# A decoder trunk on one core: experts sorted by load, the four smallest in half-width unsplit products

## What is computed

```python
D_FF = 3584; N_EXPERTS = 8; TOP_K = 2
def swiglu(h, wg, wu, wd):
    return (jax.nn.silu(h @ wg) * (h @ wu)) @ wd
def moe_swiglu(h, router, wg, wu, wd):
    logits = (xt @ router).astype(jnp.float32)          # 256 tokens x 8 experts
    topv, topi = lax.top_k(logits, TOP_K)
    gates = jax.nn.softmax(topv, axis=-1)
    ...
    xb = xpad[row_tok].reshape(n_blocks, MOE_BLOCK, d)  # tokens grouped by expert
    yb = lax.map(expert_block, (xb, block_expert))      # swiglu with that expert's weights
    y = (yb.reshape(n_rows, d) * row_gate[:, None]).astype(h.dtype)
    out = jnp.zeros((t + 1, d), h.dtype).at[row_tok].add(y)[:t]
```

## Time and profile before

| | us |
|---|---|
| three runs | 1573.34, 1575.76, 1575.86 |
| median | 1575.76 |
| profiled execution | 1574.27 |
| its span, first to last instruction | 1572.4 |
| busy: PE, VectorE, ScalarE, GpSimd | 1555.0, 1264.7, 1073.2, 81.7 |
| expert stage, first to last product | 613.84 to 1564.65 |

### The profile page before, as it was taken

The page is one execution under the profiler, slowest core; times in us unless marked ns, Lnnn a source line. Parts: engine busy times, 40 slices in busy tenths (PEclk is TensorE's granted clock), DMA queues, the critical chain, the costliest instruction groups (busy, mean ns, idle before and its releaser), DMA issues.

```text
span 1572.4 us, 28661 instructions
## 1 busy us (share of the span) xinstructions
PE 1555.0 (99%) x10958; PEld 1360.2 (87%) x10958; DVE 1264.7 (80%) x1448; ACT 1073.2 (68%) x1323; POOL 81.7 (5%) x82
## 2 busy tenths in 40 slices
PE   8999999999999999999999999999999999999997
PEld 8989999999998898888888888888888888888886
DVE  5686754444558867999999999999999999999996
ACT  5545544444446455888888888888888888888885
POOL 0022000000000400000000000000000000000000
PEclk9999999999999999999999999999999999999999
DMA  8700555555344017999999999999999999999994
GB/s 314 235 2 3 229 198 177 178 184 188 123 182 134 3 38 301 394 372 358 400 381 353 416 381 351 401 381 347 419 382 348 402 382 358 399 385 360 397 379 153
DMA packets 66808, 447.76 MB, mean 285 GB/s; under 512 B 8208, under 2 KB 10784, under 8 KB 14112
## 3 DMA queue, kind: packets, MB, share of 16 engines
q1 hardware_dynamic: 63344, 434.46, 71.7%
q0 software_dynamic: 2688, 9.44, 2.8%
q10 hardware_dynamic: 688, 2.62, 0.5%
HBM read 438.63 MB, written 6.29 MB: 283 GB/s over the span
## 4 chain that ended last, share of the span: by engine, by line
PE 96%; DVE 2%; ACT 1%; issue 1%; DMA 0%; POOL 0%; SPq 0%; DVEq 0%; ACTq 0%; POOLq 0%
PE bank L790 28%; PE bank L792 27%; PE bank L791 27%; PE bank L771 9%; PE bank L1465 2%; ACT w_hi L1544 0%; DMA ring<-in_w_in 0%; PE bank L961 0%; PE bank L811 0%; PE bank L1428 0%; PE bank L1214 0%; DVE w_lo L1986 0%; PE bank L1106 0%; POOL out L741 0%; ACT arena L1544 0%
## 5 line engine op out<-in xcount | busy, mean ns | idle before, releaser
L1544 ACT ACTIVATE w_hi<-ring 128x1024 fp32r<-128x1024 f32 x812 | 858.1, 1061 | 328.4 <-PE bank L792 320.3
L2247 DVE TENSOR_TENSOR w_lo<-ring,w_hi 128x1024 fp32r<-128x1024 f32 x672 | 813.5, 1224 | 60.5 <-ACT w_hi L1544 11.3
L790 PE MATMUL bank<-w_hi,acts_hi 128*128 128x512 f32 (+1 forms) x1376 | 538.9, 392 | 0.2 <-DVE w_lo L2247 0.2
L792 PE MATMUL bank<-w_hi,acts_lo 128*128 128x512 f32 (+1 forms) x1376 | 533.1, 387 | 0.0
L791 PE MATMUL bank<-w_lo,acts_hi 128*128 128x512 f32 (+1 forms) x1376 | 532.3, 387 | 0.0
L792 PEld LDWEIGHTS bank<-w_hi,acts_lo 128*128 128x128 f32 x1376 | 258.4, 188 | 53.6
L790 PEld LDWEIGHTS bank<-w_hi,acts_hi 128*128 128x128 f32 x1376 | 258.6, 188 | 51.6 <-DVE w_lo L2247 0.9
L791 PEld LDWEIGHTS bank<-w_lo,acts_hi 128*128 128x128 f32 x1376 | 258.7, 188 | 50.7
L790 PE MATMUL bank<-acts_hi,w_hi 128*128 128x256 f32 x884 | 252.5, 286 | 1.8 <-DVE acts_lo L2176 0.8
L791 PE MATMUL bank<-acts_lo,w_hi 128*128 128x256 f32 x884 | 250.1, 283 | 0.0
L792 PE MATMUL bank<-acts_hi,w_lo 128*128 128x256 f32 x884 | 250.0, 283 | 0.0
(11 more groups left out here) (247 smaller groups left out, 1113.2 us busy)
## 6 DMA issues: line engine op xcount, KB each, us to landing
ring<-in_moe_wg SPq DMA_DIRECT2D x112, 1024.0 KB, 6.5
ring<-in_moe_wu SPq DMA_DIRECT2D x112, 1024.0 KB, 6.4
ring<-in_moe_wd SPq DMA_DIRECT2D x112, 1024.0 KB, 6.8
ring<-in_w_in SPq DMA_DIRECT2D x24, 1024.0 KB, 7.1
ring<-in_dense_wg SPq DMA_DIRECT2D x14, 1024.0 KB, 4.7
ring<-in_dense_wu SPq DMA_DIRECT2D x14, 1024.0 KB, 4.8
ring<-in_dense_wd SPq DMA_DIRECT2D x14, 1024.0 KB, 4.8
ring<-in_w_o SPq DMA_DIRECT2D x8, 1024.0 KB, 6.3
```

The lines of the kernel that those rows point to most:

```text
L790: pe.matmul(out_, a_hi, b_hi, start=first, stop=False, **kw)
L792: return pe.matmul(out_, a_lo, b_hi, start=False, stop=final, **kw)
L1544: return act.activation(o, i, ACT.Copy, **kw)
L2247: TT(w_lo[:, q, :], raw, w_hi[:, q, :].bitcast(F32), ALU.subtract).then_inc(lo_ready, 1)
```

## The change

The experts are ordered on chip by their load: expert 0 first, whatever its load (its weights are already being loaded when the order is known), then by falling load. They are taken in four pairs. The first of a pair (expert 0 and the three fullest) is computed as before, with 128 seats. The second (the four emptiest) gets 64 seats, and its products take the float32 weights as they are in the ring and unsplit activations. The stationary operand has 64 columns then, and two products stand side by side in the array: g in columns 0 to 63 and u in 64 to 127, each into its half of the partitions of one bank; and for the down products the two halves of the output columns. SyncE loads g and u of such an expert alternately, half by half, since PE uses them together, and a slot is free when PE has read it (`raw_read`). Which expert's weights are loaded is read by SyncE from `order_id` in SBUF. An expert that doesn't fit into its seats sets `flag`, and `over_pass` takes all eight again. The four pairs are a loop of three passes and a last pair.

```diff
+        EXPERT_B = []
+        for _j in range(NJ):
+            EXPERT_B += [(kind, _j, hf) for hf in range(2) for kind in "gu"]
+            EXPERT_B += [("d", _j - 1, hf) for hf in range(2) if _j]
+        EXPERT_B += [("d", NJ - 1, hf) for hf in range(2)]
...
+            def pair_pass():
+                for r in range(PAIRS):
+                    e = sp.value_load(order_id[0:1, 2 * r:2 * r + 1], min_val=0, max_val=NE - 1) if r else 0
+                    for i in range(PER_E):
+                        if i >= SLOTS:
+                            sp.wait_ge(lo_ready, MOE0 + r * PIECES_E + 2 * (i - SLOTS + 1))
+                        elif r:
+                            sp.wait_ge(raw_read, r * PER_E + i - SLOTS + 1)
...
+                        load_expert(e, i)
+                    if r == 0:
+                        sp.wait_ge(flag_ready, 1)
+                    e = sp.value_load(order_id[0:1, 2 * r + 1:2 * r + 2], min_val=0, max_val=NE - 1)
+                    for i in range(PER_E):
+                        if i >= SLOTS:
+                            sp.wait_ge(raw_read, r * PER_E + i - SLOTS + 1)
...
+                        load_expert(e, i, EXPERT_B)
...
+            def half_columns(j, hf, seen):
+
+                slots = []
+                for kind in "gu":
+                    i = place_b[(kind, j, hf)]
+                    pe.wait_ge(ring_in[e_slot[i]], seen.fills + e_count[i])
+                    slots.append(half_cols(e_slot[i]))
+                for k in range(4 * hf, 4 * hf + 4):
+                    for g, w in enumerate(slots):
+                        last_ = pe.matmul(bank[j % 2][g * C:(g + 1) * C, :], xb[:, k, :], w[:, k % 4, :],
+                                          start=k == 0, stop=k == KT - 1, skip_group_check=True)
+                last_.then_inc(raw_read, 2)
...
+            def down_rows(j, hf, seen):
+
+                i = place_b[("d", j, hf)]
+                pe.wait_ge(ring_in[e_slot[i]], seen.fills + e_count[i])
+                for q in (2 * hf, 2 * hf + 1):
+                    w = half_rows(e_slot[i])[:, q % 2, :]
+                    for g in range(2):
+                        last_ = pe.matmul(bank[4][g * C:(g + 1) * C, :], act_t[j % 2][:, q, :],
+                                          w[:, g * CW:(g + 1) * CW], start=j == q == 0, stop=j == NJ - 1 and q == 3,
+                                          skip_group_check=True)
+                last_.then_inc(raw_read, 1)
+
+            def half_chunks(seen):
+
+                for j in range(1, NJ):
+                    half_columns(j, 0, seen)
+                    turn_half(j - 1, seen)
+                    half_columns(j, 1, seen)
+                    pe.wait_ge(ac_ready, seen.acts + j)
+                    down_rows(j - 1, 0, seen)
+                    if j == NJ - 1:
+                        turn_half(j, seen)
+                    down_rows(j - 1, 1, seen)
+
+            def pair(r, last_one):
+
+                full, half_ = full_seen(r), half_seen(r)
+                full_chunks(full)
+                turn_half_slots(r * 32 + 16)
+                down(NJ - 1, full)
+                pe.wait_ge(ga_kept, half_.turned_x + 1)
+                for hf in range(2):
+                    half_columns(0, hf, half_)
+                pe.wait_ge(yg_kept, full.outs + 2)
+                half_chunks(half_)
+                if not last_one:
+                    turn_slots(full_seen(r + 1), r * 32 + 32)
+                pe.wait_ge(ac_ready, half_.acts + NJ)
+                for hf in range(2):
+                    down_rows(NJ - 1, hf, half_)
+                if not last_one:
+                    column_chunk("g", 0, full_seen(r + 1))
+                    column_chunk("u", 0, full_seen(r + 1))
+                    pe.wait_ge(yg_kept, half_.outs + 1)
```

More of the change, by code:

```diff
@@ L1 @@
+from collections import namedtuple
 from contextlib import ExitStack
@@ L66 @@
 N_PARAM = _at
+PAIRS = NE // 2
+Seen = namedtuple("Seen", "pieces fills turned_x low_x acts turned turned_kept silus outs experts halves raws")
 def constant_tables():
@@ L1775, in dense_split, with split @@
                         hi_ready, 1)
-            def split(kind, j, at1, pieces=range(4)):
+            def split(kind, j, seen, pieces=range(4)):
                 for q in pieces:
@@ new lines, in keep_out @@
+            def keep_out(seen, halved=False):
+                if not halved:
+                    act.wait_ge(pc_free, seen.pieces + (MOE0 + PIECES_E + PIECES))
+                act.wait_ge(gate_ready, seen.experts + 1)
+                act.wait_ge(to_set, seen.experts + 1)
+                for hf in range(2):
+                    if halved and hf == 0:
+                        act.wait_ge(half_done, 1)
+                    if halved and hf:
+                        act.wait_ge(pc_free, seen.pieces + (MOE0 + PIECES_E + PIECES))
+                    act.activation(yg[:, hf * 512:(hf + 1) * 512], bank[4 + hf][:, :], ACT.Identity,
+                                   scale=gate_e).then_inc(yg_kept, 1)
@@ new lines, in keep_half_out, with pair @@
+            def keep_half_out(seen):
+                act.wait_ge(raw_read, seen.halves + PER_E)
+                act.wait_ge(gate_ready, seen.experts + 1)
+                act.wait_ge(to_set, seen.experts + 1)
+                act.activation(yb, bank[4][:, :], ACT.Identity, scale=gate_e).then_inc(yg_kept, 1)
+            def pair(r, last_one):
+                full, half_ = full_seen(r), half_seen(r)
+                full_chunks(full)
+                half_x(half_)
+                keep_out(full)
+                keep_raw(0, half_)
+                for j in range(1, NJ):
+                    half_silu(j - 1, half_)
+                    keep_raw(j, half_)
+                half_silu(NJ - 1, half_)
+                if not last_one:
+                    gathered(full_seen(r + 1))
+                    split("g", 0, full_seen(r + 1))
+                keep_half_out(half_)
+                if not last_one:
+                    split("u", 0, full_seen(r + 1))
+                    silu(0, full_seen(r + 1))
```

685 lines of the change are left out of this document (402 added, 283 removed).

## The result

The changed kernel takes **1548.3 us** (median of four runs, 1547.4 to 1549.4) against 1575.3 us: a ratio of 0.983, interval 0.981 to 0.985. It is faster by 27 us where 67 were forecast. The sign was right, and so was what bounds a half expert; two fifths of the size came.

A forecast was written before the change was run, and what follows sets the result against it. PE bounds the kernel and loads follow it. Four pairs of about 219.5 us (878), plus 4.7 at the start and 1.7 at the end, make 885 for a 950.8 us stage: 66 off 1574.27 gives 1508 us, range 1485 to 1535 (0.63).

The forecast's parts named there:

- what bounds a half expert: In each 64-seat expert, loads set the pace: 105 us of loads against 79 us of PE work.
- forecast 420: Load rate taken for the 64-seat experts: 420 GB/s, read where loads caught up in the old trace.
- restart (3.2): After a 64-seat expert the ring is empty, so PE stands about 3.2 us before the next 128-seat expert.
- Rival (a): In 64-seat experts the two column groups don't overlap: 1716 us, slower; chance 0.09 together with all of Rival (b).
- Rival (b): PE's clock falls in 64-seat experts: 1530 to 1550 us if mixed; all of it, with Rival (a), 0.09.
- Rival (d): An expert with 64 seats has more tokens, so a second pass over eight runs: 948 us more; chance 0.01.
- rival (c): Loads hardly faster than before: 1538 us at 400 GB/s, 1572 at 381 (no change, 0.03), 1594 at 372 (worst, 0.03).
- the full part: The 128-seat expert of a pair, at PE's pace: 118.5 us, 121.7 with PE's standstill at its start.
- the scatters: Writing rows out at expert boundaries slows the loads: 1.4 us for each scatter, two in a pair.
- the queue is idle for 3: In the 128-seat expert's 121.7 us the ring lets some 46 loads through, 118.7 us, leaving the queue idle for 3.
- The sum: Time of a pair in terms of loads: 216.3 us with scatters, plus idle queue, about 219.5; bounds 216 and 227.
- the start: In the first expert PE waits once for VectorE's added ordering and gate steps: 4.7 us, bounds 0 and 6.

The follow-up runs named there:

- run 5: Changed kernel with both products of each pair in the 64-seat experts on the same 64 columns instead of side by side: 1727.2 us, 1.097.
- run 4: Changed kernel with every second gate, up and down product of the 64-seat experts left out, loads and waits kept: 1532.5 us, 0.973.
- Run 6: Changed kernel with the 64-seat expert's row transposes and first 16 products moved ahead of the preceding expert's last down products on TensorE: 1539.2 us, 0.977.
- run 1: Changed kernel with the loop over pairs written out on TensorE, ScalarE and VectorE: 1534.0 us, 0.974.
- run 2: Changed kernel with the loop over pairs written out on TensorE alone: 1534.9 us, 0.976.
- Run 3: Kernel before the change, with TensorE's loop over single experts made to hold two per turn: 1585.4 us, 1.007.
- run 8: Kernel of run 1 with the work that orders the experts removed, so they run as 0 to 7: 1529.6 us, 0.973.
- run 7: Changed kernel with the edits of run 1 and Run 6 together: 1532.2 us, 0.975.
- Run 12: Changed kernel with run 1's and Run 6's edits, order steps behind every second split, later TensorE waits and slot products, two more throwaway products: 1520.6 us, 0.966.

## Why the prediction was right and wrong

**Right: what bounded the kernel, and what would bound a half expert.** Loads at 412 to 421 GB/s in half experts (forecast 420), PE busy 80% there (75 to 85), records 0.22 us apart in a shared group, g and u side by side (run 5), 2.3 to 3.1 us of idle PE at the restart (3.2), half the splits. Rival (a) was priced at 1716 and measured at 1727. Rival (b) was rightly small: the clock did fall in some groups, to 0.91 to 0.96 over a half expert, and in run 4, with half of the products, 0.77 cost no load time. Such a group, behind a wait for its load, took 5.35 us for 3.65:

```profile
771.29 5.35 PE L1593 MATMUL bank<-ring,arena 128*64 128x512 f32 x16 [2.53 <-DMA ring<-in_moe_wu]
```

The Trainium skill warns of a low clock in groups of products that are shorter than the wait for their load ("TensorE: Matmul & The Clock Gate", HAM oscillation — how this bites in real kernels). Here the group is longer than its wait, 3.65 against 2.53 us, and yet some groups ran slow; it cost no load time. Rival (d) didn't happen, and rival (c) not as it was put: the half expert's slots were enough for 421 GB/s. The Trainium skill's 358 GB/s for one core ("DMA: Bandwidth & Descriptors", Specifications), by which the time would have been 1632 by the prediction's estimate, is not what this core drew. The 425 that the same page of the Trainium skill has for a core alone (Bandwidth) is near the 421 of the trace.

As a mean over a whole pair, though, the loads ran at 89.7 MB in 232.3 us, or 386 GB/s. So the time fell among 1535 to 1570, which had a chance of 0.18, for loads at 390 to 402 or a falling clock; what was lost was lost in the full part and at the hand-over, which no rival named. Rival (c)'s times are also added up unevenly: 1538 at 400 GB/s has the scatters in it, 1572 at 381 has not, and would be 1583 with them.

**Wrong: "the queue is idle for 3".** This is the term that was mis-sized most: with the scatters 5.8 us of load time were to be lost in a pair, and 18.9 were, of which some 5 go with the jump, told below. A full part was to let 46 loads through. But when PE restarts at 851.39, two of them have landed already, or just then. ScalarE's first two splits of g come from one load and the next two from another:

```profile
848.95 2.00 ACT L1695 ACTIVATE w_hi<-ring 128x1024 fp32r<-128x1024 f32 x2 [3.55 <-DMA ring<-in_moe_wg]
851.42 2.01 ACT L1695 ACTIVATE w_hi<-ring 128x1024 fp32r<-128x1024 f32 x2 [0.47 <-DMA ring<-in_moe_wg]
```

And 120 us at 383 GB/s are 46.0 MB, fewer than 44 loads. That this is why the full part lost so much was argued, and no run tested it. The other place was tested. Behind VectorE's last split of the full expert (739.9) no slot comes back until PE's first raw read of the next (748.6):

```profile
737.51 2.36 DVE L2445 TENSOR_TENSOR w_lo<-ring,w_hi 128x1024 fp32r<-128x1024 f32 x2 [0.24 <-ACT w_hi L1695]
746.47 0.15 DVE L2775 COPY arena<-arena 128x1 f32 x1 [6.59 <-ACT arena L2089]
```

Two loads are queued for 8.7 us, and the queue runs dry. The sum counted slots and forgot when each is given back. By the stretches 8.3 us of load time go in that place in the second pair. Run 6 filled most of the gap and got 2.3 and 3.9 us in the second and third pair for it, so not all of the lost load time was lost time: the full part is still at PE's pace.

**Missing: the jump.** No step of the sum looked at the length of TensorE's loop body, which the change made a third longer (637 to 864 instructions). It costs a stall of 3.6 to 4 us at two boundaries and a low clock behind it (0.79 over the 8 us from 866 and from 1098, where run 1 has 1.00): 14.2 us by the median of run 1, 13.4 by run 2's. The periods name 5.4 and 4.9 of it; 2.8 more in run 1's trace are the gather at the start, which varies between traces of the same code there. Run 3 lost 10 us by two such jumps. So some 10 of the 40.2 us missing in the stage are the jump's, the largest single piece that a run recovered.

**Too small, by the traces: the start.** 4.7 us forecast, of which 4.2 for what run 8 leaves out; 7.4 by its trace, but 4.4 by the medians and 1.7 by the ratios. The waits were about right, the clock that falls behind a wait wasn't counted. The stage also begins 1.15 us later (614.99 for 613.84).

With the jump and the gap gone a pair takes 223 to 225 us, 3.5 to 5.4 over the forecast. In run 7 the loads keep 393 GB/s for 120 us and 350 for the next 16, so 10.4 us of load time are still lost there where the sum had 5.8; no run took that apart. Run 12, with all edits, has a stage of 898.3 us (610.55 to 1508.81): of the 40.2 us missing 26.3 are won back, by runs that each had a cause in view, and 13.9 stay open.

## What to carry to other kernels

When a kernel hands over from one consumer of a ring to another, write down when each slot is given back, not how many there are: a pause in the giving back shows up in the load rate one queue length later. Before a loop's body grows, look at whether the trace shows instruction transfers inside the loop; here, once it did, every jump back cost a stall of 3 to 4 us plus the low clock behind it, and writing the loop out removed it. A resource found idle in one half of a period and full in the other is worth less than its average idle time.

## What the runs showed that was not expected

- TensorE's loop body ran free of instruction transfers at 637 and 780 listed instructions and needed 16 KB pieces at 864 and 1274; at a jump back TensorE then stood for 3.1 to 4.3 us (the changed kernel, runs 3, 5 and 6). Written out, the code was fetched as well, without a stall (run 2).
- Behind a pause of 1.28 or 1.29 us the same 32 records took 3.84 us in four traces and 5.3 to 6.6 in the others, at a granted clock from 608 to 612 of 1.00 and of 0.50 to 0.63. With 0.9 us of the pause filled the one trace had 3.84, and the kernel's spread was 3.7 us and not 10 (run 12); that the filling did it isn't shown.
- One core's loads ran at 421 GB/s for 96 us on end.
